# Three of the eight plain one-hots of a routing block made by ScalarE instead of GpSimd

## The reference, cut to what matters

```python
s1, i1 = lax.top_k(s[:, :, 0], K)          # K = 16
s2, i2 = lax.top_k(s[:, :, 1], K)
cand = (s1[..., :, None] + s2[..., None, :]).reshape(T, H, K * K)
sc, ci = lax.top_k(cand, K)
e1 = jnp.take_along_axis(i1, ci // K, axis=-1)
e2 = jnp.take_along_axis(i2, ci % K, axis=-1)
idx = e1 * PEER_NKEYS + e2
g = jax.nn.softmax(sc, axis=-1)
...
a = jnp.einsum('cd,chkd->chk', xc, u[ic])
act = jax.nn.gelu(a) * gc
out = jnp.einsum('chk,chkd->cd', act, v[ic])
```

## Time and profile before

| | |
|---|---|
| median of 3 runs | 4077.91 us (4076.83 to 4078.27) |
| the profiled execution | 4077.23 us |
| its span in the trace | 4075.9 us |
| PE busy | 3880.0 us (95%) |
| DVE busy | 2196.0 us (54%) |
| ACT busy | 1485.0 us (36%) |
| POOL busy | 527.0 us (13%) |
| the routing's blocks, in the trace | from 2560 us to 3098 us |

### The profile page before, as it was taken

One profiled execution on the slowest core, in us unless ns is written; L12 is line 12 of the kernel. 1 busy time (PEld: TensorE's weight loads), 2 busy tenths in 40 slices (PEclk: granted clock), 3 DMA queues, 4 the chain that ended last, 5 costly groups with the idle time before them and its releaser, 6 DMA issues.

```text
span 4075.9 us, 48842 instructions
## 1 busy us (share of the span) xinstructions
PE 3880.0 (95%) x20256; PEld 3102.1 (76%) x20256; DVE 2196.0 (54%) x3862; ACT 1485.0 (36%) x1871; POOL 527.0 (13%) x748
## 2 busy tenths in 40 slices
PE   7998999999899899999899999999999999999999
PEld 4755788888775578877777878777878888888887
DVE  3274553333548464464553356888954666654444
ACT  3245532122234632224553433344434222222222
POOL 0000000000000000000002000577773111100000
PEclk9999999999999999999999999999999999999999
DMA  5400113333120022231114233445446665643332
GB/s 214 160 9 1 63 63 116 112 119 126 57 75 1 32 82 94 94 131 66 64 40 146 73 119 121 141 153 162 166 164 216 194 193 180 197 137 114 114 124 83
DMA packets 109838, 459.84 MB, mean 113 GB/s; under 512 B 9216, under 2 KB 43120, under 8 KB 68912
## 3 DMA queue, kind: packets, MB, share of 16 engines
q1 hardware_dynamic: 82048, 354.96, 24.4%
q0 software_dynamic: 27568, 101.74, 8.4%
HBM read 389.04 MB, written 67.63 MB: 112 GB/s over the span
## 4 chain that ended last, share of the span: by engine, by line
PE 84%; DVE 7%; ACT 5%; DMA 2%; POOL 2%; issue 1%; DVEq 0%; SPq 0%; ACTq 0%; POOLq 0%
PE ps L607 23%; PE ps L608 23%; PE ps L609 23%; PE ps L2652 2%; PE ps L1269 1%; DVE ACC L1470 1%; PE ps L688 1%; PE ps L513 1%; DVE MX L1443 1%; POOL OH L2788 1%; PE ps L1348 1%; PE ps L2198 1%; PE ps L2217 1%; PE ps L2425 1%; PE ps L1287 1%
## 5 line engine op out<-in xcount | busy, mean ns | idle before, releaser
L607 PE MATMUL ps<-HH,WH 128*128 128x512 f32 x2760 | 1060.0, 384 | 38.2 <-DVE HL L915 19.6
L608 PE MATMUL ps<-HL,WH 128*128 128x512 f32 x2760 | 1045.4, 379 | 0.0
L609 PE MATMUL ps<-HH,WL 128*128 128x512 f32 x2760 | 1042.0, 378 | 0.0
L484 DVE TENSOR_TENSOR WL<-stage,WH 128x2048 fp32r<-128x2048 f32 x244 | 558.9, 2290 | 449.8 <-ACT WH L473 449.7
L473 ACT ACTIVATE WH<-stage 128x2048 fp32r<-128x2048 f32 x244 | 465.2, 1907 | 531.4 <-PE ps L609 484.7
L607 PEld LDWEIGHTS ps<-HH,WH 128*128 128x128 f32 x2760 | 525.3, 190 | 147.6 <-issue 42.5
L609 PEld LDWEIGHTS ps<-HH,WL 128*128 128x128 f32 x2760 | 523.7, 190 | 104.1
L608 PEld LDWEIGHTS ps<-HL,WH 128*128 128x128 f32 x2760 | 525.3, 190 | 97.8 <-issue 1.2
L607 PE MATMUL ps<-AHp,WH 128*128 128x512 f32 x1024 | 405.4, 396 | 0.0
L608 PE MATMUL ps<-ALp,WH 128*128 128x512 f32 x1024 | 405.3, 396 | 0.0
L609 PE MATMUL ps<-AHp,WL 128*128 128x512 f32 x1024 | 405.3, 396 | 0.0
(11 more groups left out here) (425 smaller groups left out, 4913.5 us busy)
## 6 DMA issues: line engine op xcount, KB each, us to landing
stage<-in_w SPq DMA_DIRECT2D x64, 1024.0 KB, 4.8
stage<-in_u SPq DMA_DIRECT2D x64, 1024.0 KB, 4.8
stage<-in_v SPq DMA_DIRECT2D x64, 1024.0 KB, 4.8
stage<-in_w_mod SPq DMA_DIRECT2D x42, 1024.0 KB, 4.8
GR<-gdram POOLq DMA_DIRECT2D x32, 1024.0 KB, 8.0
AR<-adram POOLq DMA_DIRECT2D x88, 256.0 KB, 3.4
adram<-GR SPq DMA_DIRECT2D x21, 1024.0 KB, 5.1
gdram<-GST SPq DMA_DIRECT2D x16, 1024.0 KB, 5.6
```

Source lines behind the costliest of these rows:

```text
L484: dve.e.tensor_tensor(k.WL[o % 2][:, 0:w], k.stage[n % 2][:, 0:w], k.WH[o % 2][:, 0:w].bitcast(F32), ALU.subtract).then_inc(*dve.done("sla ...
L607: pe.e.matmul(o, wh[:, kk, cs], L.hh[:, kk, z], start=first, stop=False)
L608: pe.e.matmul(o, wh[:, kk, cs], L.hl[:, kk, z], start=False, stop=False)
L609: mm = pe.e.matmul(o, wl[:, kk, cs], L.hh[:, kk, z], start=False, stop=last)
```

## The change

ACT makes the last 3 of the 8 plain one-hots of each block, and POOL the first 5. ACT does it in two steps: three times |n - e2| for n = 0..127 (`Abs`, with the negated index as a bias per partition), and then relu(1 - that) over all three at once. For n and e2 whole numbers this is 1 where they are equal and 0 elsewhere. ACT also makes `NE`, the negated copy of `E2`, with each tile's `chosen`. PE waits for `hot2a` in addition to `hot1` and `hot2`.

```diff
@@ memory
     k.E1, k.E2, k.GG = k.ta[0][:, 0:512], k.ta[1][:, 0:512], k.td[0][:, 0:512]
+    k.NE = k.td[1][:, 0:512]
@@ tensor_route
                 pe.wait_ge("hot1", (tt, b))
                 pe.wait_ge("hot2", (tt, b))
+                pe.wait_ge("hot2a", (tt, b))
@@
+BY_SCALAR = 3
@@ scalar_route
                 op = act.e.activation(dst[:, 128 * tt:128 * tt + 128],
                                       k.psn.of(("chosen", tt))[:, 128 * c:128 * c + 128], ACT.Copy)
+            op = act.e.activation(k.NE[:, 128 * tt:128 * tt + 128], k.psn.of(("chosen", tt))[:, 128:256], ACT.Copy, scale=-1.0)
             op.then_inc(*act.done("chosen", tt))
...
+        if kind == "spread" and i < 16:
+            oh = k.OH.of((tt, i))
+            if i >= 3 or tt > 0:
+                act.wait_ge("g_mm", (tt, i - 3) if i >= 3 else (tt - 1, i + 13))
+            act.wait_ge("chosen", tt)
+            act.wait_ge("iota", 0)
+            for t in range(8 - BY_SCALAR, 8):
+                tok = 128 * tt + 8 * i + t
+                op = act.e.activation(oh[:, 1, t, :], k.IO[:, :], ACT.Abs, bias=k.NE[:, tok:tok + 1])
+            op.then_inc(*act.done("apart", (tt, i)))
+            act.wait_ge("apart", (tt, i))
+            act.e.activation(oh[:, 1, 8 - BY_SCALAR:8, :], oh[:, 1, 8 - BY_SCALAR:8, :], ACT.Relu, bias=k.ones[:, 0:1],
+                             scale=-1.0).then_inc(*act.done("hot2a", (tt, i)))
@@ pool_route
-            for t in range(8):
+            for t in range(8 - BY_SCALAR):
```

More of the change, by code:

```diff
@@ L45 @@
     "dilated_evicted": ("mg", "ds_exp", "ds_turned", "yd"),
-    "route_evicted": ("qp", "keys", "g_exp", "chosen", "g"),
+    "route_evicted": ("apart", "hot2a", "qp", "keys", "g_exp", "chosen", "g"),
     "mix_evicted": ("z_act", "m_hi", "y", "relu", "act_hi", "down0"),
```

## The result

| | before | changed |
|---|---|---|
| median of 11 runs | 4078.27 us (4076.43 to 4082.07) | 4087.43 us (4085.47 to 4092.32) |
| the profiled execution | 4077.23 us | 4087.64 us |
| its span | 4075.9 us | 4086.3 us |

The ratio of changed to before is 1.0022, 95% interval 1.0014 to 1.003. So the change costs some 9 us, where 0.7 was forecast, and the time lies 0.4 us above the range.

What follows compares the result with a forecast made beforehand. PE was taken as the bound, busy 3880.0 of 4075.9 us. Tile ends of -1.2, -0.65 and +2.5 us, clock 0, gave +0.65 on 4077.23; with 0.68 to the median, 4078.6 us, range 4070 to 4087.

Steps and rivals of the forecast that it cites:

- What bounds the kernel, and POOL's wait: PE, busy 3880.0 of 4075.9 us; its 12.3 us of waits for POOL would end, the wait for `picked` staying behind them.
- A: Tile end at 2695 us: PE waits for POOL, then `picked`; transposes forecast 1.2 us earlier.
- C: Tile end at 2969 us: PE waits for POOL, then `picked`; transposes forecast 0.65 us earlier.
- d = 1.6 us a block: ACT's added time per block for three Abs and one Relu: 1.6 us, bounds 1.1 to 2.0, no table load.
- What DVE gains: Between exponential and `picked`, DVE runs faster with POOL less at work: 0.5 us, bounds 0 and 1.0.
- The ends: Sum over three tile ends: -1.2 us at A, -0.65 us at C, +2.5 us at B.
- B: Tile end at 2828 to 2835 us: PE waits for DVE alone, first `hot1`, then `picked`; forecast 2.5 us later.
- The second term of 1.1 us for `GST` at B: SP's half waits behind a slab that waits for DVE's WL, so `GST` is free and the copy starts 1.1 us later.
- the ring: Loop of delays, not named in the prediction: `GST` half, ACT's copy, one-hots, WH, WL, slab, next `GST` half.
- Delays to DVE earlier in the tile ... vanish in those 3.76: Late WH delays DVE by at most 3.2 us, absorbed by DVE's 3.76 us wait for the exponential at A.
- The clock, 0 give or take 1 us: PE's half-clock stretches after each wait stay, begun later over other matmuls: 0 us, give or take 1.
- ACT's lateness counts twice: Rival: WH late by twice d also at A and C holds DVE; up to +11.4 us, 4090 us; chance 0.07.

Runs made afterwards that it cites:

- SP's half first: Changed kernel with SP sending its half of `GST` ahead of the same call's weight slab: 4080.85 us; the same edit in the kernel before: 4077.84 us.
- the two parts: Against the kernel before: ACT's added work into an unread buffer, POOL making all eight, 4083.22 us; POOL making five, three left out, ACT nothing, 4074.79 us.
- ACT's part alone: Against the kernel before: ACT does its Abs and Relu into a scratch buffer nobody reads, POOL makes all eight one-hots; 4083.22 us, ratio 1.001.

## Why the prediction was wrong, step by step

- *What bounds the kernel, and POOL's wait.* Right. It is gone, and behind it stands the choice, with one wait of 6.78 and 6.79 us at A and C, where 6 to 7 were forecast.
- *d = 1.6 us a block.* Right, 1.5: from copy to WH it was 2767.08 - 2765.22 = 1.86 us and is 2769.13 - 2765.77 = 3.36. The Trainium skill ("ScalarE: Activation LUTs", Table sets: the hidden batching unit) says that relu and abs are in every set, and the trace agrees: the 260 new instructions are 64 times four and four `NE`, so no load came.
- *What DVE gains.* The size of one instruction was right, and it is small: at end A L2780 takes 2.98 us with POOL at work and 2.76 with POOL idle, as in the earlier trace rows.
- *The ends.* The transposes at A come 1.3 us earlier against the first ones, where 1.2 was forecast. The third tile is 0.5 us longer, where 0.65 shorter was forecast; the slow stretch behind B's second wait, 1.6 us costlier, accounts for that. The first wait at B was to grow by 2.5 us and grew by 0.26, because PE itself came later, held by the wait for WL and the slow clock ahead of it. The second term of 1.1 us for `GST` at B was the ring itself; I wrote it down for one place and didn't run it through the tile. The second tile as a whole took 5.3 us more, where 2.5 was forecast; 2.5 of the 5.3 are the clock's.
- *"Delays to DVE earlier in the tile ... vanish in those 3.76".* This step failed. It asked when `picked` is done and not who else waits for WL. PE reads each WL, with 1.0 us to spare in the second tile, and SP's queue passes the delay on to the next copy. Cost: 2.1 us of waiting in the second tile, 3.1 at the end of the fourth and after, where I had looked at no row. Cutting the ring in two different places took the wait for WL away both times. The wait at the fourth tile's end is not the ring's: SP's half first leaves it, the one-hots ahead of the copy and POOL's eight in tile 3 take it away.
- *The clock, 0 give or take 1 us.* Failed as well: 3.6 us. The waits stayed, and another slow stretch came behind the one at 3103 (1.7 us lost), but those at A and at B's second wait also grew longer: 2.6 us lost in place of 1.8, and 3.0 in place of 1.4. The sum has a fault of its own here. It takes A's gain at the transposes. Before the change A's slow stretch lay ahead of them, so that gain already counts its end; with the change it lies behind them and adds to what follows, so "begun later" could not be free.
- *The rivals.* "ACT's lateness counts twice" named the right engine and the right direction, at the ends; the loss was in between. It had 0.07, too little for a mechanism of which I had found one link (WH late, WL late) and called the rest covered without reading the cover's size off PE's rows.

**Open.** Why the slow stretches are longer no run tells. That the two parts don't add up is explained for A and C, and at the fourth tile's end as far as the landings of `GST` go.

## What to carry to other kernels

When work moves to an engine with room, don't ask how much room it has but where in its queue it stands still, and put the work ahead of that wait: three one-hots ahead of the copy took 4076.1 us, behind it 4087.4. Follow a delay past the next engine, through every queue that sends or frees a buffer (SP's too), until it comes back or ends in a wait whose length you have read; if it comes back, it can add up (here it did so once). The best kernel here, three one-hots ahead of the copy, is 2.8 us faster than before, 0.1% (0.01 to 0.19%): a wait of 12.3 us for POOL had another of nearly the same length behind it.

## What the runs showed of the hardware

- A short wait may or may not cost clock. Windows of the changed kernel, with the granted clock ahead of the last two numbers: 2 us behind the end of the wait at A, then right behind the 2.10 us at 2797, then 1.4 us behind the 1.99 us at 3103.

```profile
2698.60:2700.60 2.00, 2.00 (x6) 1.54 (x5) 2.00 (x8) 0.00 (x0) 2.00 (x4) 0.50 1.04 382
...
2797.50:2799.50 2.00, 2.00 (x9) 1.63 (x10) 2.00 (x9) 1.97 (x5) 0.00 (x0) 1.00 0.45 127
3104.50:3106.50 2.00, 2.00 (x9) 1.81 (x9) 0.00 (x0) 1.02 (x2) 0.00 (x0) 0.50 0.29 123
```

  The clock stays at 2.4 GHz behind the wait at 2797 and is 1.2 GHz behind the two others. With ACT's part alone the wait at 2797 was 2.41 us, and there 1.7 us were lost at half clock. The length alone doesn't decide it: with the one-hots ahead of the copy, the 16 records behind a wait of 3.31 us (at 2826.19) all ran at 2.4 GHz, in 2.02 us.
- Where the blocks begin differs between profiled executions though nothing ahead of them was touched: the first transposes lie between 2557.1 and 2564.6 us. So a single span tells nothing below some 5 us; the account above is safe because it counts from a fixed point of the program.
- POOL's one-hot took 0.729 us on the mean in the kernel before and 0.715 in the changed one (0.735 and 0.680 for those in `Y`). The mean hides a spread: in the kernel before, eight of them took 8.93 us from 2669.97, 1.12 each, with DVE at WL, one-hots and a compare of 128x2048, and eight took 4.75 us from 2776.72, 0.59 each, with DVE mostly at its searches for the largest values.
- A slab of 1 MB sent close to the halves of `GST` lengthens their landing: 9.6 to 9.9 us with the slab 3.4 us ahead, 11.4 to 12.0 with it 0.4 us behind (the kernel before and the same with SP's half first, fourth tile).
